# Second LayerNorm moved into the expert loop of a two-layer hybrid decoder step, on one Trainium2 core

## The reference

```python
xp = layer_norm(DEEPNORM_ALPHA * xp + mix, ln1_g[l], ln1_b[l])
xp = layer_norm(DEEPNORM_ALPHA * xp + hier_moe(xp, *moe_w), ln2_g[l], ln2_b[l])

def hier_moe(x, ...):            # 4 groups of 8 experts
    ...                          # best group, then the best two of its 8 experts
    h = silu(xb @ w_gate[e]) * (xb @ w_up[e])     # 1024 -> 512, gated
    return h @ w_down[e]                          # 512 -> 1024
```

## Time and profile before

| | |
|---|---|
| median of 3 runs | 2220.56 us (2220.1 to 2220.86) |
| time of the profiled execution | 2221.0 us |
| its span, first to last instruction | 2219.2 us |
| TensorE busy | 2058.5 us (93%) |
| VectorE, ScalarE, GpSimd busy | 704.0, 382.3, 298.3 us |
| mean granted TensorE clock | 0.956 of full |
| moved by DMA | 527.44 MB, mean 238 GB/s |

### The profile page before, as it was taken

One profiled execution on the slowest core, in us unless ns is written; L12 is line 12 of the kernel. 1 busy time (PEld: TensorE's weight loads), 2 busy tenths in 40 slices (PEclk: granted clock), 3 DMA queues, 4 the chain that ended last, 5 costly groups with the idle time before them and its releaser, 6 DMA issues.

```text
span 2219.2 us, 31577 instructions
## 1 busy us (share of the span) xinstructions
PE 2058.5 (93%) x12532; PEld 1233.7 (56%) x12532; DVE 704.0 (32%) x1370; ACT 382.3 (17%) x984; POOL 298.3 (13%) x312
## 2 busy tenths in 40 slices
PE   8999999989999999989599999999999989998990
PEld 5666655566555655545366666555765546544550
DVE  4412166671111111111482123767411111111116
ACT  2001123301211111111110111332011111211110
POOL 1200011111111111111331000110011111110104
PEclk9999999999999999989799999999899999998995
DMA  6610013358999999999434110223689999999964
GB/s 226 182 39 29 19 42 116 133 199 317 366 379 383 402 366 382 375 378 345 170 115 115 38 39 11 90 79 130 262 340 367 381 390 380 376 377 372 380 260 158
DMA packets 75368, 527.44 MB, mean 238 GB/s; under 512 B 14554, under 2 KB 23642, under 8 KB 50290
## 3 DMA queue, kind: packets, MB, share of 16 engines
q1 hardware_dynamic: 62162, 491.52, 57.5%
q0 software_dynamic: 13056, 33.84, 6.2%
HBM read 486.21 MB, written 54.60 MB: 244 GB/s over the span
## 4 chain that ended last, share of the span: by engine, by line
PE 88%; DVE 5%; issue 4%; ACT 1%; DMA 1%; POOL 0%; DVEq 0%; SPq 0%; POOLq 0%
PE ps L570 19%; PE ps L869 18%; PE ps L912 10%; PE ps L710 9%; PE ps L865 5%; PE ps L857 5%; PE ps L551 4%; PE ps L840 3%; PE ps L906 2%; PE ps L919 2%; PE ps L891 2%; PE ps L754 1%; PE ps L800 1%; PE ps L657 1%; PE ps L681 1%
## 5 line engine op out<-in xcount | busy, mean ns | idle before, releaser
L570 PE MATMUL ps<-arena 128*128 128x344 f32 x1440 | 421.1, 453 | 0.0
L871 PE MATMUL ps<-arena 128*64 128x256 f32 x1792 | 418.1, 389 | 0.0
L869 PE MATMUL ps<-arena 128*64 128x256 f32 x1792 | 418.0, 389 | 0.0
L570 PEld LDWEIGHTS ps<-arena 128*128 128x128 f32 x1440 | 272.0, 190 | 142.9 <-issue 3.6
L869 PEld LDWEIGHTS ps<-arena 128*64 128x64 f32 x1792 | 237.0, 135 | 164.7 <-issue 23.6
L912 PE MATMUL ps<-arena 128*64 128x512 f32 x448 | 241.4, 689 | 54.7 <-issue 54.6
L914 PE MATMUL ps<-arena 128*64 128x512 f32 x448 | 241.8, 690 | 0.0
L871 PEld LDWEIGHTS ps<-arena 128*64 128x64 f32 x1792 | 236.4, 134 | 0.0
L1830 POOL DMA_INDIRECT ytok<-arena,gidx x64 | 94.0, 1468 | 986.6 <-ACT arena L1165 374.2
L1606 DVE SCALAR_TENSOR_TENSOR arena<-ps,gates,arena 64x256 f32<-64x256 f32 (+1 forms) x128 | 61.1, 477 | 475.2 <-ACT arena L1142 475.2
L710 PE MATMUL ps<-arena 128*128 128x512 f32 x448 | 195.9, 594 | 4.8 <-ACT arena L1090 4.8
(11 more groups left out here) (243 smaller groups left out, 2079.9 us busy)
## 6 DMA issues: line engine op xcount, KB each, us to landing
arena<-in_w_gate SPq DMA_DIRECT2D x64, 2048.0 KB
arena<-in_w_up SPq DMA_DIRECT2D x64, 2048.0 KB
arena<-in_w_down SPq DMA_DIRECT2D x64, 2048.0 KB
arena<-in_w_in SPq DMA_DIRECT2D x36, 512.0 KB, 3.5
arena<-out_y_all SPq DMA_DIRECT2D x16, 512.0 KB, 3.5
xs<-arena SPq DMA_DIRECT2D x16, 512.0 KB, 2.7
ytok<-arena SPq DMA_DIRECT2D x16, 512.0 KB, 3.6
arena<-ytok SPq DMA_DIRECT2D x16, 512.0 KB, 7.5
```

The lines of the kernel that those rows point to most:

```text
L570: last = mm(ps[:, 3 * half + ch, 0:CH], wring[:, slot, k * P:(k + 1) * P], xT[:, k, ch * CH:(ch + 1) * CH], start=(k == 0), stop=(k == KD ...
L869: mm(ps[HALF:P, 2 + q, 0:256], xgT[:, slot, k, 0:HALF], wg_half[slot3][q][:, k], start=(k == 0), stop=(k == KD - 1))
L871: last = mm(ps[0:HALF, 2 + q, 0:256], xgT[:, slot, k, 0:HALF], wu_half[slot3][q][:, k], start=(k == 0), stop=(k == KD - 1))
```

## The change

The second LayerNorm is taken out of stage 5 and done inside the expert loop, for each turn two turns later.

- The routing also finds, for each token, which of its two turns comes first and which last (`visits`: 16 operations on VectorE, and 18 matmuls of 64 columns on TensorE, placed behind the first `gate_up`; a few small ones around them), as two index columns for each turn (`visit`), the index outside the range where a row is not meant.
- In turn e VectorE adds the output to the gathered x1 rows in the token buffer (`summed`). GpSimd writes the rows for which this is the first visit to `ytok[0]` by a plain scatter (`part_scatter`), waits for its landing, and then reads over the buffer the stored partial sums of the rows for which it is the last visit (`part_gather`).
- Two turns later VectorE adds the output again (`whole`), takes the statistics (`statistics2`) and normalises the rows (`shifted`, `normalised2`), with `inverse` on GpSimd, and GpSimd scatters the rows of a last visit straight to `y_all` (`final_scatter`). In the last turn all partial sums are read before the output is added.
- There are six token buffers instead of two, four of them over `lnp[:, 0:2]` (the first LayerNorm's parameters), `cosT` and `sinT`. The tables are loaded again before layer 1.
- Stage 5 goes. Before layer 1 SP waits for all final scatters and loads `y_all` in nine tiles. With overflow a branch does the old stage 5.

```diff
-                def scatter(e, slot, turn, col, rows, turn_other):
...
-                                         in_=ys[0:rows, slot], in_offset=None, compute_op=ALU.add,
+                def part_gather(e):
+                    rows = rows_of(e)
+                    pool.wait_ge(s["part_out"], 16 * (NE * l + min(e, NE - 2) + 1))
+                    pool.wait_ge(s["xg_mm"], BASE + NE * l + e + 3)
...
+                def part_scatter(e):
+                    rows = rows_of(e)
+                    pool.wait_ge(s["sum_done"], BASE + NE * l + e + 1)
...
+                def final_scatter(e):
+                    rows = rows_of(e)
+                    pool.wait_ge(s["l2_done"], BASE + (NE - 1) * l + e)
...
+                for e in range(NE - 2):
+                    if e > 2:
+                        inverse(e - 2)
+                    part_scatter(e)
+                    if e > 2:
+                        final_scatter(e - 2)
+                    if e + 3 < NE:
+                        next_gather(e + 3)
+                    if e:
+                        part_gather(e)
...
+                def summed(e):
+                    n = NE * l + e
+                    r, x = slice(0, rows_of(e)), xgs[e % NXG]
+                    dve.wait_ge(s["y_a"], BASE + n + 1)
+                    dve.wait_ge(s["y_d"], BASE + n + 1)
...
+                    v.tensor_tensor(x[r], x[r], ys[r, e % 2], ALU.add).then_inc(s["sum_done"], 1)
+
+                def whole(e):
+                    n = NE * l + e
+                    r, x = slice(0, rows_of(e)), xgs[e % NXG]
+                    dve.wait_ge(s["part_in"], 16 * ((NE - 2) * l + e))
+                    dve.wait_ge(s["sum_done"], BASE + n + 1)
+                    v.tensor_tensor(x[r], x[r], ys[r, e % 2], ALU.add).then_inc(s["whole_done"], 1)
...
                 def y_evict(e, slot, rows):
...
-                    act.wait_ge(s["ys_free"], BASE + n + 1)
+                    act.wait_ge(s["whole_done"], BASE + (NE - 2) * l + max(e - 2, 0))
...
-                for t in range(NT):
-                    sp.dma_start(xin[t][0:tile_rows(t)], a["ytok"][0, t * P:t * P + tile_rows(t), :]
-                                 ).then_inc(s[f"l2_in{t}"], 16)
...
+                for n in range(NXG):
+                    sp.wait_ge(s[f"ln_out{n}"], 16 * FINAL_ON_SLOT[n] * (l + 1))
                     settle(sp, s["sp_passed"])
...
+                if l < DEPTH - 1:
+                    for t in range(NT):
+                        sp.dma_start(xin[t][0:tile_rows(t)], a["y_all"][l + 1, t * P:t * P + tile_rows(t), :]
+                                     ).then_inc(s[f"l2_in{t}"], 16)
+                    sp.dma_start(cosT[:], a["c_cos"]).then_inc(s["const_in"], 16)
+                    sp.dma_start(sinT[:], a["c_sin"]).then_inc(s["const_in"], 16)
```

More of the change, by code:

```diff
@@ L925, in pair @@
                     gate_up(e, 0, slot3[0], turn3[0], first, m)
+                    if e == 0:
+                        visits()
                     hidden_turned(e, 0, first, m)
-                    gathered(e + 1, 1, turn, second)
+                    gathered(e + 1, second)
                     hidden_turned(e, 1, first, m)
@@ L1590, in xg_evict, with hidden @@
                                   ).then_inc(s["xg_d"], 1)
-                def hidden(e, col, rows, turn=None):
+                def hidden(e, rows, turn=None):
                     n = NE * l + e
+                    col = place(e)
                     if rows == MID:
@@ new lines, in _ @@
+                xg_evict(0, 0, P)
+                visits()
+                for e in range(NE):
+                    rows = rows_of(e)
+                    hidden(e, rows, (e // 2 - (0 if e < 2 * EARLY_PAIRS + 2 else 1)) if rows == MID else None)
+                    ht_evict(e, rows)
+                    if e < NE - 1:
+                        xg_evict(e + 1, (e + 1) % 2, rows_of(e + 1))
+                    if e == 0:
+                        visit_rows()
+                    late = NE - 2 if e == NE - 1 else e - 2
+                    if late > 0:
+                        whole(late)
+                        statistics2(late)
+                    if e == NE - 2:
+                        shifted(late)
+                        normalised2(late)
+                    y_evict(e, e % 2, rows)
+                    summed(e)
+                    if e == NE - 2:
+                        whole(e - 1)
+                        statistics2(e - 1)
+                    elif e == NE - 1:
+                        statistics2(e)
+                        for done in (e - 1, e):
+                            shifted(done)
+                            normalised2(done)
+                    elif late > 0:
+                        shifted(late)
+                        normalised2(late)
@@ L1865, in _ @@
+                inverse(NE - 4)
+                final_scatter(NE - 4)
+                part_scatter(NE - 2)
+                inverse(NE - 3)
+                part_gather(NE - 2)
+                part_gather(NE - 1)
+                final_scatter(NE - 3)
+                inverse(NE - 2)
+                inverse(NE - 1)
+                final_scatter(NE - 2)
+                final_scatter(NE - 1)
+                part_scatter(NE - 1)
                 pool.wait_ge(s["rk_done"], BASE + l + 1)
```

403 lines of the change are left out of this document (256 added, 147 removed).

## The result

The changed kernel took 2229.21 us (median of 6 runs) beside 2220.33 us for the one before on the same chip, a ratio of 1.0045 with an interval of 1.0035 to 1.0055. It is slower by 0.45%, where 1.4% faster was forecast. The profiled execution took 2229.5 us, its span is 2227.7, 8.5 longer than before.

What follows compares the result with a forecast made beforehand. TensorE was taken to set the pace before 576 us, the DMA engines from then on. The terms summed as 2221.0 - 31 + 0 + 9.3 - 9 = 2190.3, or 2190 us, with a forecast range of 2176 to 2204.

Steps and rivals of the forecast that it cites:

- Which resource sets the pace: Expert loops: TensorE sets the pace before 576 us, the DMA engines from then on.
- Tail of layer 1, -31: Last output copy to the end: tail falls from 50.1 to 19 us, -31 us, between -34 and -29.
- Between the layers, 0: Layer 0's last output copy to layer 1's first projection: later load, shorter way after it, 0 us, between -4 and +6.
- Routing, +9.3: Routing of both layers: `visits` matmuls 4.05 us plus small operations 0.6, 4.65 us a layer, +9.3, between +2 and +10.
- VectorE and GpSimd in the loop, 0: Expert loop: added work and waits for partial sums just fit, with 0.7 us of room for `hidden`, 0 us.
- DMA in the loop, -9: Expert loops: 21.1 MB of plain rows a layer at 3.0 us/MB replace accumulating ones, -9 us, between -24 and +30.
- Rival E, 2232: Expert loop: lag of two turns too short, late landings stall VectorE and TensorE, 2232 us at the maxima; chance 0.10.
- Rival D, 2218: Expert loop: bytes, not engine time, set the pace, DMA term +19 instead of -9, 2218 us; chance 0.08.
- The range and chances: Whole kernel: 8 in 10 between 2168 and 2213 us; faster 0.85, no change 0.05, slower 0.10.

Runs made afterwards that it cites:

- e4: The kernel before with its scatter no longer accumulating, so the sum over a token's two experts is left out: 2181.54 us, 0.9833 of before.
- i1: The kernel before with one more indirect gather per turn, reading 4 KB rows 8 apart into a buffer nobody reads: 2346.65 us, 1.0561 of before.
- e2: The changed kernel with a lag of three turns instead of two and the partial gather one turn later: 2238.83 us, 1.0085 of before.
- e3: The changed kernel with a lag of three turns, the partial gather staying in its own turn: 2239.35 us, 1.0100 of before.
- e1: The changed kernel with the partial gather reading xs1 into its own buffer, so it waits for no scatter: 2232.09 us, 1.0062 of before.
- f1: The changed kernel with VectorE's partial-sum addition, statistics and second normalisation on a few columns only: 2215.38 us, 0.9992 of before.
- g1: The changed kernel with only the partial gather's rows skipped, the partial scatter staying: 2172.17 us, 0.9783 of before.
- f2: The kernel before with two more indirect gathers per turn whose rows are all skipped: 2236.22 us, 1.0087 of before.
- f3: The changed kernel with every row of the partial scatter and partial gather skipped, instructions kept: 2149.89 us, 0.9686 of before.
- f4: The changed kernel without the instructions of the partial scatter and partial gather: 2145.98 us, 0.9675 of before.
- i3: The kernel before with one more plain indirect scatter per turn, writing 4 KB rows to an unread part of ytok: 2269.88 us, 1.0215 of before.
- h: The kernel before with each choice's rows scattered plainly to their own place and added after the loop: 2209.91 us, 0.9953 of before.

## Why the prediction was wrong

Point by point, by its own steps.

- **Which resource sets the pace.** Right. The loops follow the engine time of the two queues: e4's loop fell 20.0 us for 18.9 of engine time, i1's rose 62.3 for 64.7. A loop is 22 to 28 us longer than the two queues' time; only e2 (33.1) and e3 (30.2) stand out.
- **Tail of layer 1, -31.** Right: 19.2 us, forecast 19, and `part_in` was late as argued (VectorE waited 1.9 us for turn 30's).
- **Between the layers, 0.** The first projection came at T + 25.0 (26 forecast), since the load started at T + 13.5 instead of T + 16. Up to the new parts of layer 1's routing the piece was 7.0 us shorter: 1.3 of that earlier start; 2.5 in the first projection, which took 7.39 us at a granted clock of 0.50 in its first half and now takes 4.86 at 1.00; and 3.2 of the chance dip shown above. So the change gave -3.8, at the edge of the -4 to +6, and the clock's part of it wasn't in the forecast.
- **Routing, +9.3.** Right: `visits` took 3.96 us (4.05), the rest 1.45 (0.6); +5.3 in layer 0, +4.8 in layer 1, together 10.1.
- **VectorE and GpSimd in the loop, 0.** Right in its result. VectorE did wait for `part_in` (18.3 us in the loop of layer 0) and GpSimd's turn did take 16.9 us, more than the 15.6 that it must fit in; e1 to e3 and f1 show that this cost little or nothing.
- **DMA in the loop, -9.** This step failed. Its own quantity was exact: q0 5.8% and 42.33 MB, 3.0 us/MB. What failed is that it counted only q0's packets: "now two gathered, one written plainly, one read back, one written to `y_all`" were all given one price per MB, and q1's packets were taken to stay as they were. Measured, in a layer's stretch from turn 1 to 31: no accumulation, -19 us (e4); 1,032 rows read back, +29.5 (g1), of which 17.9 on q1, where the forecast had nothing; 5,080 more skipped rows at 14 to 19 ns, +5. Sum +16, measured +17.1. The term is +36 for both loops instead of -9, and that is the miss: with all terms as measured, 2221.0 - 30.9 - 7.0 + 10.1 + 36.3 = 2229.5.
- **Rival E, 2232.** Its number was nearly the result by luck, its mechanism wasn't at work: the gathers of tokens took up to 18.6 us in the loop instead of 14.1, but the two landings that it added up took 11.5 to 13.5 and 12.4 to 13.2, some 25 us together, where it needed more than 28.9. VectorE and GpSimd stood, and taking the round trip away changed nothing.
- **Rival D, 2218.** Bytes didn't set the pace: the stretch carried 342 GB/s in i1, 358 in the change, 376 in e4, all with the engines taken for 95 to 96% of it. And its term, +19, was half of the +36. The Trainium skill's page "SBUF — State Buffer", section "Summary: rules for kernel authors", reckons with about 358 GB/s; the changed kernel's stretch happens to have that figure, but g1's has 370 and e4's 376, with the same weights.
- **The range and chances.** The price of plain rows was bounded by 2.6 and 4.07 us/MB of q0. Both bounds were about the queue's own packets; a bound on what it does to the other queue was missing, and 10 in 100 for slower was too little.

What stays open: why a row read from DRAM to SBUF lengthens the weights' packets and a row written doesn't. The weights are themselves read from DRAM to SBUF, so both queues may want the same side of an engine; that is a guess, and no run here looks inside one. The Trainium skill's page "DMA: Bandwidth & Descriptors", section "Queues, rings and completion order", says that an engine takes its queues in turn, packet by packet. That fits the shares of the two queues, which add up to 94 to 96% in every loop here, and would not by itself tell reads from writes. It is also open why the same read row cost 457 ns in g1 and 404 in i1. Nor was it tried whether larger rows than 4 KB are read more cheaply.

## What to carry to other kernels

When the DMA engines set the pace, price a transfer by what it adds to all queues: here 400 to 460 ns of engine time for a 4 KB row read beside the weights, 146 to 181 for one written, 172 more for one accumulated, 14 to 19 for one skipped. So trading an accumulating write for a plain write and a read back loses, and trading it for two plain writes to two places wins in the loop. A wait that a change brings with it (for tokens, for a landing) says who comes last and not what sets the pace: first take the share of both queues times the length, and see whether the sum explains the loop.

## What was not expected of the hardware

- The same 175.5 MB of weights took 440 to 472 us of engine time depending on how much GpSimd's queue read beside them besides the tokens, and 440 to 445 whatever it wrote, skipped or accumulated (e4, f2, f3, f4, g1, i3, h).
- Skipping rows is nearly free for the engines, but two more indirect transfers a turn made the whole kernel before 19 us slower (f2). TensorE's wait there is for tokens (29.6 us at L842) instead of for weights, and what makes the tokens late was not tested.
- VectorE at 265 us busy or at 141 (f1) made no difference to the packets' times.
